# Eighteen steps of a projection moved from a serial phase to a phase of gathers

## The chip, the cores and the metric

The kernel runs on one core of a Trainium2 chip. The metric is the time of one execution on the device in microseconds (us). TensorE is PE in the views (PEld is its weight load), VectorE DVE, ScalarE ACT, GpSimd POOL, SyncE SP.

## The reference

One layer of a streaming encoder for 1024 prompt tokens and 128 sample tokens (8 streams of 16), 1152 in all. Cut to what matters:

```
h  = rms_norm(x, norm1_g);  z = h @ w_in           # columns: rq rk rv rg fq fk fv (512 each), ff (8)
ro = retention(rotary(rq), rotary(rk), rv, state)
fq = rms_norm(fq, fox_qn_g); fk = rms_norm(fk, fox_kn_g); logf = log_sigmoid(ff + b_f)
fo = softmax(fq @ fk.T / 8 + cumulated logf, causal) @ fv
x  = x + concat(norm(ro) * silu(rg), norm(fo)) @ w_out
q  = norm(x) @ wq;  s1, s2 = q halves @ keys       # 8 heads, 2 x 128 keys
e  = the 16 best of the 16 x 16 sums of the 16 best of s1 and of s2;  g = softmax of them
x  = x + sum over 8 x 16 experts of g * gelu(norm(x) . u[e]) * v[e]
```

Outputs are x, the new keys fk, the new values fv, logf and the new retention states. All arithmetic is in float32.

## The kernel before, in words

The 1152 tokens are 9 tiles of 128: tiles 0 to 7 the prompt, tile 8 the samples. The program is a row of phases, each with its own instruction stream for every engine: `phase_norm` (h, transposed, kept in SBUF as `hT`), `projection([RQ, RK, RV])`, `phase_retention`, `projection([RG, FQ, FK, FV])` (the second projection), and `phase_tail`.

A projection takes its groups of 512 columns one after the other and in each the 9 tiles: eight float32 matmuls of 128x512 on PE (L332, each recorded as two passes), and for FQ and FK a square on ACT (L385), a sum per head on DVE (L483), a power on POOL (L418), two multiplications on DVE (L502, L512), and four transposes on PE (L309), copied by ACT. Queries and keys (transposed) go to the scratch tensors `qts` and `kts`, new keys and values to the outputs. The weights of a group (2 MB) sit in one of two buffers. The phase ends when all its stores have landed.

`phase_tail` does everything else, in three groups of three tiles. Its main work is 1152 gathers, each an indirect DMA on POOL's queue (L1256) that brings one row of `peer_uv` (u and v, 8 KB) to each of 128 partitions, into a ring of nine buffers. For each, DVE makes a dot product (L1882); for each four, DVE and ACT make the weights and PE adds the v halves into PSUM (L1641, `yp`), which frees four buffers for POOL. Beside this main work each group has front steps: attention (names fox...), output projection (h...), routing (r...: queries against keys L1594, the best 16 of each half, and the choices `choose`, L1705 on). The choices of a tile end with its indices moved by ACT (L1305); the first gather of the tile waits for these, and the fifth gather of all waits for the last scores of group 0. Groups 1 and 2 are worked among the gathers.

The order is fixed when the program is built. `front_steps` lists the front steps in two threads (`rest` and `choice`) with a cost on each engine and what each needs; `deal` plays a planner's clock in which a gather lands every 2.52 us and puts each step between two items of the main work of its engine. In the second thread each choice is cut in 33 pieces (CAND). The buffers `cand` and `oh` of the choices lie over `fq`, the attention's queries, so `loadq` of group 1 waits until the choices of group 0 are done; attention of group 1 starts after that. SP works through its own list in order: loads, stores, and waits in between.

Of the kernel before, what the change touches and what calls it, by code (L numbers as in the profile page):

```python
# [12 lines left out]
ALU = mybir.AluOpType  # L13
# [19 lines left out]
def emit(nc, a):  # L33

    ctx = ExitStack()
    with ctx:
# [187 lines left out]
        def projection(groups):  # L224
            def body(block, sem, ps):
                steps = [(g, t) for g in groups for t in range(TILES)]
# [10 lines left out]
                if with_ff:  # L237
                    sq_done, ss_done, rs_done, rg_done = sem("sq_done"), sem("ss_done"), sem("rs_done"), sem("rg_done")
                    pool_step, gate_exp, out_done = sem("pool_step"), sem("gate_exp"), sem("out_done")
                    ff_in, ff_done, ff_z, ff_abs = sem("ff_in"), sem("ff_done"), sem("ff_z"), sem("ff_abs")  # L240
# [14 lines left out]
                def _(sp):  # L255
# [9 lines left out]
                    outs = 0  # L265
                    for n, (g, t) in enumerate(steps):
# [29 lines left out]
                    if outs:  # L296
                        sp.wait_ge(out_done, 16 * outs)

                @block.tensor
                def _(pe):  # L300
# [23 lines left out]
                    for n, (g, t) in enumerate(steps):  # L324
                        gi = n // TILES
# [9 lines left out]
                        if t == TILES - 1:  # L335
                            pe.wait_ge(z_done, n + 1)
                            pe.sem_inc(w_used, 1)
# [16 lines left out]
                def _(act):  # L354
# [46 lines left out]
                    if with_ff:  # L401
                        act.wait_ge(tr_done, len(order) + 1)
                        nc.scalar.copy(lgfT[:, 0:NP_TOK], ffpt[:, :, :].rearrange("h a n -> h (a n)")).then_inc(ffT, 1)
                        act.wait_ge(tr_done, len(order) + 2)
                        nc.scalar.copy(lgfT[:, NP_TOK:], ffpt[:, 0, 0:P])
# [298 lines left out]
        CAND = 33  # L704

        def front_steps():
# [7 lines left out]
            def bank(names, engine, name):  # L714
# [4 lines left out]
                return held  # L719

# [37 lines left out]
            for g in range(GROUPS):  # L758
                lo, hi, nt = FIRST[g], FIRST[g + 1], len(tiles_of(g))
                routed = [("pe", ("rscore", g - 1, 4 * GT - 1))] if g else []  # L760
                chosen = [("dve", ("rgate", g - 1, GT - 1))] if g else []
                if nt < GT:
# [91 lines left out]
                for i in range(GT):  # L854
                    top = ("rtop", g, 4 * i + 3 if g == 0 else n - GT + i, 4)
                    for p in range(CAND):
                        add(choice, ("rcand", g, i, p), dve=(1.15, ("dve", top)))
# [9 lines left out]
        def deal(threads):  # L867
# [8 lines left out]
            landed, dots, tanh, freed = [], [], [], []  # L876

# [41 lines left out]
            while True:  # L919
# [20 lines left out]
                if th is not None:  # L940
# [4 lines left out]
                    done[(e, name)] = start + parts[e][0]  # L945
                    continue
                did[e] += 1
                if e == "pool":
                    free[e] = start + 1.25
                    landed.append(max(start + 4.0, (landed[-1] if landed else 0.0) + 2.52))  # L950
# [12 lines left out]
                else:  # L963
                    free[e] = start + 0.1
            assert all(at[e][th] == len(queue[e][th]) for e in engines for th in range(len(threads)))
            return due

        def phase_tail(block, sem, ps):
# [23 lines left out]
            cand = M[:, 34304:36352].rearrange("p (h n) -> p h n", h=PH)  # L992
            oh = M[:, 36352:38400].rearrange("p (k j) -> p k j", j=TOPK)
# [10 lines left out]
            qbd = S[:, 5904:6928].rearrange("p (r b a q) -> p r b a q", r=PAIRS, b=NB, a=2)  # L1004
            ckT = S[:, 6928:7952].rearrange("p (r n) -> p r n", r=PAIRS)
            pn, pns = S[:, 7952:8224], S[:, 8224:8496]
            psT = S[:, 8496:8880].rearrange("p (j m) -> p j m", j=3)
            foT = S[:, 8880:9392].rearrange("p (r n) -> p r n", r=PAIRS)
            lfs, cs, ones_s = S[0:64, 9392:9664], S[0:64, 9664:9936], S[0:64, 9936:10208]
# [17 lines left out]
            ssum = S[:, 5888:5896]  # L1027
            keys2 = S[:, 5904:6928].rearrange("p (s i n) -> p s i n", s=2, i=4)
# [16 lines left out]
            mins = sb("mins", [P, 4])  # L1045
            lsum = sb("lsum", [P, GT, NH])
# [18 lines left out]
            so_mm, so_ev, fT_mm, fT_ev = (sem(x) for x in ("so_mm", "so_ev", "fT_mm", "fT_ev"))  # L1065
            w_in, g2_in = [sem(f"w_in{k}") for k in range(KC)], sem("g2_in")
# [15 lines left out]
            def _(sp):  # L1082
# [9 lines left out]

                def load_wout(g):
# [3 lines left out]
                def front(step):  # L1097
                    kind, g, arg = step[0], step[1], step[2:]
                    if kind == "load":
                        w = (tiles_of(g)[-1] + 1) * P  # L1100
                        if g:
                            sp.wait_ge(s_mm, 4 * GT * g)
                        if len(tiles_of(g)) < GT:
# [917 lines left out]
```

## Time and profile before

| | us |
|---|---|
| median of 3 runs | 4134.53 |
| lowest and highest | 4133.03, 4137.62 |
| the profiled execution | 4142.67 |
| its span (first to last instruction on the core) | 4140.9 |
| mean granted clock of TensorE | 0.731 of full speed |

The profile tells of one execution. Its sections used here are the busy tenths in 40 slices, the queues, the groups of instructions, the windows and the timelines. Times in views count from the start of the span. Busy shares are averages over stages with different limits: up to about 1014 us the engines work through serial phases, after it the gathers run.

### The profile page before, as it was taken

The numbers are of one execution on the slowest core, as the hardware profiler recorded it, in microseconds if no ns is written. First come the engines' busy times: TensorE is split into PE (matmuls) and PEld (weight loads), VectorE is DVE, ScalarE is ACT, GpSimd is POOL, SyncE is SP. The second block draws the span as 40 slices with busy tenths as digits, with TensorE's granted clock in tenths as the row PEclk, the third lists the DMA queues.
The fourth block names the chain that finished last, engine by engine and source line by source line (L and its number), as shares of the span: only waits on it lengthen the run. The fifth ranks groups of instructions, "written<-read, shape, count | busy, mean of one in ns | idle before, by whom it ended". The sixth has DMA issues, their size and how long they took to land.

```text
span 4140.9 us, 34632 instructions
## 1 busy us (share of the span) xinstructions
PE 2460.3 (59%) x11906; PEld 1033.4 (25%) x11906; DVE 2506.7 (61%) x6235; ACT 472.9 (11%) x1311; POOL 1375.9 (33%) x1257
## 2 busy tenths in 40 slices
PE   7998996885337755774753467557734334334333
PEld 3465443442003322321320033123201001001000
DVE  3201720138886655687768766557898875555555
ACT  1000111211002200110110122001101000000000
POOL 0000220001444343433334443433444444444443
PEclk9965997698557777886666588778866565656655
DMA  3001034112999999999989999999999999999999
GB/s 109 21 11 53 21 102 168 69 41 116 420 414 409 421 418 418 394 411 397 413 346 419 416 404 421 420 418 404 412 409 414 418 415 417 421 417 418 416 421 371
DMA packets 242304, 1347.92 MB, mean 326 GB/s; under 512 B 33472, under 2 KB 47624, under 8 KB 94672
## 3 DMA queue, kind: packets, MB, share of 16 engines
q0 software_dynamic: 165888, 1208.03, 70.8%
q1 hardware_dynamic: 73936, 135.34, 8.9%
q10 hardware_dynamic: 2304, 2.32, 0.2%
q8 instruction: 95, 1.56, 0.2%
q14 instruction: 81, 0.66, 0.0%
HBM read 1318.40 MB, written 27.21 MB: 325 GB/s over the span
## 4 chain that ended last, share of the span: by engine, by line
DMA 38%; PE 18%; DVE 14%; POOL 7%; issue 5%; ACT 1%; SPq 1%; another core or an unknown queue 0%; POOLq 0%; DVEq 0%; ACTq 0%
DMA M<-in_peer_uv,M 38%; PE yp L1641 11%; POOL M L1256 7%; DVE M L1882 6%; PE ab L1594 2%; DVE exg L1899 1%; PE ef L1629 1%; DVE strips L1904 1%; PE c L1573 1%; PE d L1480 1%; PE ab L1457 1%; PE d L1573 1%; DVE gel L1891 1%; DVE M L1693 1%; DVE gel L1893 1%
## 5 line engine op out<-in xcount | busy, mean ns | idle before, releaser
L1256 POOL DMA_INDIRECT M<-in_peer_uv,M x1152 | 1294.3, 1123 | 1954.7 <-PE yp L1641 1493.5
L1882 DVE SCALAR_TENSOR_TENSOR M<-M 128x1024 f32<-128x1024 f32 x1152 | 1411.1, 1225 | 870.8 <-DMA M<-in_peer_uv,M 836.2
L1641 PE MATMUL yp<-M,strips 128*32 128x512 f32 x4608 | 927.1, 948 | 1371.1 <-DVE strips L1904 1318.0
L1641 PEld LDWEIGHTS yp<-M,strips 128*32 128x32 f32 x4608 | 161.8, 147 | 2006.2 <-DVE strips L1904 1562.8
L332 PE MATMUL z<-M 128*128 128x512 f32 x1008 | 442.2, 596 | 1.4 <-PEq L104 1.0
L1418 ACT ACTIVATE gel<-gel 128x4 f32<-128x4 f32 x288 | 59.2, 206 | 2233.1 <-DVE gel L1893 2232.5
L1594 PE MATMUL ab<-M 128*128 128x512 f32 x576 | 269.7, 620 | 1.3 <-ACT M L1374 1.3
L332 PEld LDWEIGHTS z<-M 128*128 128x128 f32 x1008 | 189.5, 191 | 226.6 <-issue 226.6
L414 POOL TENSOR_SCALAR small<-small 128x8 f32<-128x8 f32 x27 | 6.1, 227 | 519.5 <-DVE small L483 519.5
L1594 PEld LDWEIGHTS ab<-M 128*128 128x128 f32 x576 | 111.1, 200 | 150.8 <-issue 149.2
L1457 PE MATMUL ab<-M 64*128 64x512 f32 (+3 forms) x192 | 98.2, 627 | 24.1 <-DMA M<-qts_scratch 20.4
L1470 PE MATMUL c<-ident,M 128*128 128x128 f32 x288 | 60.8, 328 | 73.3 <-ACT M L1291 70.7
L1904 DVE SCALAR_TENSOR_TENSOR strips<-gel,exg 128x128 f32<-128x128 f32 x288 | 84.0, 292 | 32.4 <-ACT gel L1418 22.2
L1480 PE MATMUL d<-M 128*64 128x128 f32 x576 | 102.9, 339 | 0.9 <-ACT M L1299 0.9
L1780 DVE CUSTOM_DVE_ANT_0 M<-ab,M 128x896 f32<-128x896 f32 (+6 forms) x64 | 48.2, 755 | 78.2 <-PE ab L1459 59.0
L1882 DVE DVE_READ_ACCUMULATOR M<-M 128x1 f32 x1152 | 94.7, 82 | 0.0
L1899 DVE TENSOR_TENSOR exg<-e,gel 128x128 f32<-128x128 f32 x288 | 84.0, 292 | 10.0
L1480 PEld LDWEIGHTS d<-M 128*64 128x64 f32 x576 | 82.6, 174 | 23.8 <-issue 21.1
L1629 PE MATMUL ef<-ident,M 128*32 128x128 f32 x2304 | 84.7, 296 | 5.8 <-issue 3.8
L1629 PEld LDWEIGHTS ef<-ident,M 128*32 128x32 f32 x2304 | 71.7, 120 | 26.8 <-issue 18.1
L1573 PE MATMUL c<-M 128*128 128x512 f32 x144 | 73.0, 662 | 7.0 <-ACT M L1362 7.0
L1278 ACT ACTIVATE M<-M,mins 128x896 f32<-128x896 f32 (+6 forms) x64 | 49.6, 775 | 227.8 <-DVE mins L1780 227.6
(201 smaller groups left out, 2337.0 us busy)
## 6 DMA issues: line engine op xcount, KB each, us to landing
M<-in_peer_wq SPq DMA_DIRECT2D x12, 2048.0 KB, 31.5
M<-in_peer_uv,M POOLq DMA_INDIRECT x1152
M<-in_w_in SPq DMA_DIRECT2D x7, 2048.0 KB, 9.0
M<-in_w_out SPq DMA_DIRECT2D x24, 512.0 KB, 25.9
M<-in_x_prompt SPq DMA_DIRECT2D x16, 512.0 KB, 7.2
x_scratch<-M SPq DMA_DIRECT2D x9, 512.0 KB, 7.7
xts_scratch<-M SPq DMA_DIRECT2D x9, 512.0 KB, 35.9
M<-xts_scratch SPq DMA_DIRECT2D x9, 512.0 KB
```

The lines of the kernel that those rows point to most:

```text
L332: last = nc.tensor.matmul(z[n % 3][:, :], hT[:, k, t * P:(t + 1) * P], wbuf[:, gi % 2, k, :], start=(k == 0), stop=(k == KC - 1))
L1256: nc.gpsimd.indirect_dma_start(ring[n % NR], None, a["peer_uv"], bass.IndirectOffsetOnAxis(ap=idxH[:, t % 6, s // 4, s % 4:s % 4 + 1], axis=0)
L1457: nc.tensor.matmul(s[:, c:c + w], fq[b0:b0 + 64, r, i * P:(i + 1) * P], kTg[b0:b0 + 64, r, c:c + w], start=True, stop=c + w < width)
L1470: last = nc.tensor.transpose(four(C)[:, j % 4, :], pr[:, n % 3, j * P:(j + 1) * P], ident[:, :])
L1480: last = nc.tensor.matmul(Dk[b0:b0 + 64, 0:P], vg[:, j, h * HD:(h + 1) * HD], pT[:, n % 2, j, :], start=(j == 0), stop=(j == t))
L1573: last = nc.tensor.matmul((C, Dk)[c][:, :], mT[:, t % 2, k, :], wout(g)[:, k, 512 * c:512 * c + 512], start=(k == 0), stop=(k == KC - 1))
L1594: last = nc.tensor.matmul(half_ab[i % 2], xT[:, tt, k, :], wq(g, b)[:, k, :], start=(k == 0), stop=(k == KC - 1))
L1629: last = nc.tensor.matmul(EF[32 * b:32 * b + 32, half, k * P:(k + 1) * P], xTn[:, 4 * half + k, 32 * j:32 * j + 32], ident[:, :], start=Tr ...
L1641: last = nc.tensor.matmul(yp[32 * j:32 * j + 32, 512 * c:512 * c + 512], strips[:, n % 2, j, :], ring[(4 * n + j) % NR][:, D + 512 * c:D + ...
L1882: nc.vector.scalar_tensor_tensor(out=row, in0=row, scalar=1.0, in1=xrep[:, s % 4, :], op0=ALU.mult, op1=ALU.mult, accum_out=dots[:, t % 2, ...
L1899: link(nc.vector.tensor_tensor(exg[:, :, :], bc(e32[:, :].unsqueeze(1), [P, 4, 32]), bc(g[:, 3, :].unsqueeze(2), [P, 4, 32]), ALU.mult))
L1904: nc.vector.scalar_tensor_tensor(out=strips[:, n % 2], in0=bc(g[:, 2, :].unsqueeze(2), [P, 4, 32]), scalar=1.0, in1=exg[:, :, :], op0=ALU. ...
```

## The change

What it does:

- The second projection takes FQ, FK and FV for tiles 0 to 2 alone (`tiles` = 9 for RG, 3 for each of the others). It stores the normalised, transposed rows `hT` of tiles 3 to 8 to a scratch tensor `hts`: six stores of 512 KB on SP, issued behind the load of the last weights; ACT waits for them before it overwrites part of `hT`.
- `phase_tail` gets a new block of front steps, `project`, ahead of the attention of group 1: six tiles by three column groups, 18 steps. It loads the three weight blocks (2 MB each) and the six blocks of `hts` and the two gains again, does the same arithmetic (`pmm` on PE, `pact` on ACT, `psum` and `pnrm` on DVE, `ppow` on POOL, `pturn` on PE and ACT) with two buffers for each intermediate, and stores 6 blocks of `qts`, 6 of `kts`, 6 of new keys and 6 of new values, 256 KB each.
- The load of attention's keys and values for group 1 waits for all of that.
- `cand` and `oh` are halved and lie elsewhere (partly over the routing keys): `choose` handles four heads, then the other four, in 31 pieces. For groups 1 and 2 it waits for the group's last scores. `loadq` of group 1 no longer shares memory with the choices.
- `deal` now adds time to a gather's landing for the bytes that SP's transfers bring (2.4 us per MB by a table).

The diff, cut to its core:

```diff
-        def projection(groups):
+        def projection(groups, tiles):
...
+                    if with_ff:
+                        for t in range(tiles[FV], TILES):
+                            sp.dma_start(a["hts"][t].rearrange("p (k n) -> p k n", k=KC), hT[:, :, t * P:(t + 1) * P]
+                                         ).then_inc(h_out, 16)
...
+            def project(start):
+
+                add(rest, ("pload", 0, 0), sp=(25.0, *start))
+                add(rest, ("pload", 0, 1), sp=(35.0,))
+                for j in range(PJ + 3):
+                    if j < PJ:
+                        q = j // LATE
+                        used = ("dve", ("pnrm", 0, j)) if q < 2 else ("act", ("pact", 0, j))
+                        add(rest, ("pmm", 0, j, 0), pe=(3.8, ("sp", ("pload", 0, q)), *bank("AB"[j % 2], *used)))
+                        add(rest, ("pmm", 0, j, 1), pe=(3.8,))
...
+                if g == 1:
+                    project(routed + [("dve", ("rtop", 0, 4 * GT - 1, 4))])
...
+                    if e == "sp" and landed:
+                        backlog += 2.4 * (mbytes[name[0]] + (4.7 if name[0] in ("hadd", "hxt") and name[2] == GT - 1 else 0.0))
...
+                    other = min(backlog, 2.52)
+                    backlog -= other
+                    landed.append(max(start + 4.0, (landed[-1] if landed else 0.0) + 2.52 + other))
...
+                        sp.dma_start(pw[q % 2], a["w_in"][0, :, (FQ + q) * GW:(FQ + q + 1) * GW]
+                                     .rearrange("(k p) c -> p k c", p=P)).then_inc(pw_in[q % 2], 16)
...
+                    elif kind == "pturn":
+                        m = arg[0]
+                        act.wait_ge(ptr, m + 1)
+                        if m >= 2:
+                            act.wait_ge(pt_out[m % 2], 16 * (m // 2))
+                        nc.scalar.copy(p_turn[m % 2], (C, Dk)[m % 2][:, :]).then_inc(pte, 1)
...
+                        for k in range(4 * half, 4 * half + 4):
+                            last = nc.tensor.matmul(half_ab[j % 2], hTl[i][:, k, :], pw[q % 2][:, k, :],
+                                                    start=(k == 0), stop=(k == KC - 1))
...
-        program(projection([RQ, RK, RV]))
+        program(projection([RQ, RK, RV], [TILES] * 3))
         program(phase_retention)
-        program(projection([RG, FQ, FK, FV]))
+        program(projection([RG, FQ, FK, FV], [0] * 3 + [TILES] + [TILES // 3] * 3))
```

How the order moves. PE, where the gathers begin, before. L1594, L1603 and L1612 are the last routing steps of group 0, L1641 the main work (8 matmuls for each four gathers), L1457 on the attention of group 1:

```order
L1594 MATMUL ab<-M 128x512 x8
L1641 MATMUL yp<-M,strips 32x512 x8
L1603 MATMUL c<-ident,M 128x128 x4
L1612 MATMUL d<-M 128x128 x4
L1641 MATMUL yp<-M,strips 32x512 x168
L1457 MATMUL ab<-M 128x512
L1459 MATMUL ab<-maskq,identb 128x128
```

The same place now. L1644 is `pmm` (4 matmuls for half a step), L1653 `pturn`, L1811 the main work:

```order
L1811 MATMUL yp<-M,strips 32x512 x16
L1644 MATMUL ab<-M 128x512 x12
L1811 MATMUL yp<-M,strips 32x512 x8
L1644 MATMUL ab<-M 128x512 x12
L1653 MATMUL c<-ident,M 128x128 x4
L1644 MATMUL ab<-M 128x512 x4
L1811 MATMUL yp<-M,strips 32x512 x8
L1644 MATMUL ab<-M 128x512 x4
L1653 MATMUL d<-ident,M 128x128 x4
L1644 MATMUL ab<-M 128x512 x4
L1811 MATMUL yp<-M,strips 32x512 x8
```

The 22 main pieces (88 gathers) that stood on PE ahead of the attention of group 1, 21 of them with nothing between, are now 23 (92 gathers), and the 18 steps stand among them.

ACT, around the move of the indices of tile 3, before. L1414 copies the tokens of tile 3 for its dot products and so stands at the end of tile 2; L1305 CAST is the move that gather 384 waits for; L1418 stands once for each four gathers:

```order
L1414 COPY M<-ef 128x512 x6
L1418 ACTIVATE gel<-gel 128x4
L1414 COPY M<-ef 128x512 x2
L1398 ACTIVATE M<-M 128x128
L1305 CAST M<-M 32x32 x16
L1328 COPY M<-ab 128x512 x2
```

The same move now (L1432), with L1565 in the place of L1418; the copies of tile 3 (now L1561) stand twelve main pieces, 48 gathers, further down:

```order
L1565 ACTIVATE gel<-gel 128x4
L1475 COPY M<-ab 128x512 x2
L1482 COPY M<-d 128x256
L1483 COPY M<-d 16x128
L1545 ACTIVATE M<-M 128x128
L1432 CAST M<-M 32x32 x16
L1432 COPY M<-gate 32x32 x16
```

The move came after the last piece of tile 2; now it comes well ahead of it.

## Rows read from the trace of the kernel before

**Rows 1.** The page, span, and busy tenths in 40 slices of 103.5 us.

```profile
span 4140.9 us, 34632 instructions
...
PEclk9965997698557777886666588778866565656655
DMA  3001034112999999999989999999999999999999
```

**Rows 2.** Windows by stage: length, busy us (instructions) of each engine, PE clock, DMA share, GB/s.

```profile
1014.00:1250.00 236.00, 76.92 (x341) 12.86 (x340) 191.25 (x462) 20.70 (x88) 103.16 (x91) 0.58 1.00 412
1250.00:2080.00 830.00, 549.80 (x3053) 243.86 (x3054) 571.46 (x1536) 114.53 (x300) 333.15 (x296) 0.77 1.01 410
2080.00:2100.00 20.00, 14.27 (x247) 11.42 (x245) 9.94 (x25) 11.94 (x40) 3.44 (x4) 0.84 0.23 81
2100.00:4120.00 2020.00, 939.87 (x5293) 301.18 (x5292) 1388.36 (x3360) 173.12 (x542) 863.77 (x770) 0.68 1.01 415
```

**Rows 3.** DMA queues from 1014 us to the end: packets, MB, share of the 16 engines.

```profile
q0 software_dynamic: 165312, 1203.84, 93.4%
q1 hardware_dynamic: 30704, 76.62, 6.4%
```

**Rows 4.** Timeline of PE in the second projection: start, length in us, instruction.

```profile
501.86 7.03 PE L332 MATMUL z<-M 128*128 128x512 f32 x16
508.73 0.60 PE L309 MATMUL ztp<-ident,M 128*128 128x128 f32 x4
509.17 7.03 PE L332 MATMUL z<-M 128*128 128x512 f32 x16
...
627.05 48.23 PE L332 MATMUL z<-M 128*128 128x512 f32 x112
```

**Rows 5.** DMA issues of the page: count, KB each, median us to landing.

```profile
M<-in_peer_wq SPq DMA_DIRECT2D x12, 2048.0 KB, 31.5
...
M<-in_w_in SPq DMA_DIRECT2D x7, 2048.0 KB, 9.0
...
xts_scratch<-M SPq DMA_DIRECT2D x9, 512.0 KB, 35.9
...
M<-x_scratch SPq DMA_DIRECT2D x9, 512.0 KB, 8.2
...
qts_scratch<-M SPq DMA_DIRECT2D x9, 256.0 KB, 5.2
```

**Rows 6.** Short windows around two dips of the DMA share (columns as in rows 2).

```profile
1715.00:1720.00 5.00, 5.00 (x172) 4.36 (x164) 1.40 (x4) 3.37 (x7) 0.00 (x0) 1.00 0.84 347
1720.00:1725.00 5.00, 4.33 (x32) 2.25 (x21) 4.86 (x19) 1.91 (x4) 3.08 (x2) 1.00 0.24 49
...
2080.00:2090.00 10.00, 7.97 (x196) 7.35 (x198) 3.88 (x11) 2.85 (x6) 0.00 (x0) 0.82 0.20 75
2090.00:2100.00 10.00, 6.30 (x62) 4.07 (x51) 6.06 (x14) 9.09 (x35) 3.44 (x4) 0.86 0.27 88
```

**Rows 7.** Timeline of POOL where tile 3's gathers begin; in brackets idle before and releaser.

```profile
2072.93 0.94 POOL L1256 DMA_INDIRECT M<-in_peer_uv,M  x1 [0.30 <-issue]
2095.65 0.94 POOL L1256 DMA_INDIRECT M<-in_peer_uv,M  x1 [21.78 <-ACT M L1305]
```

**Rows 8.** PE groups of 1250 to 2080 us (count, busy us, mean ns), and one busy window.

```profile
L1641 PE MATMUL yp<-M,strips 128*32 128x512 f32 x1168 | 216.5, 879 | 200.9 <-DVE strips L1904 195.1 <-issue 5.7
L1594 PE MATMUL ab<-M 128*128 128x512 f32 x192 | 90.7, 623 | 0.0
...
2650.00:2700.00 50.00, 41.35 (x155) 15.05 (x154) 31.83 (x69) 5.24 (x13) 19.96 (x19) 0.91 1.01 421
```

**Rows 9.** Groups of the second projection's FQ, FK and FV part, 501.4 to 677 us.

```profile
L418 POOL TENSOR_TENSOR small<-small,nhalf 128x8 f32<-128x8 f32 x16 | 26.4, 1648 | 1.3
L512 DVE TENSOR_TENSOR M<-M 128x512 f32<-128x512 f32 x17 | 11.8, 692 | 2.9 <-DVE M L502 0.5
...
L483 DVE TENSOR_REDUCE small<-M 128x8 f32<-128x512 f32 x16 | 11.0, 686 | 43.0 <-ACT M L385 43.0
```

More of the change, by code:

```diff
@@ L222, in emit @@
         RQ, RK, RV, RG, FQ, FK, FV = range(7)
-        def projection(groups):
+        def projection(groups, tiles):
             def body(block, sem, ps):
-                steps = [(g, t) for g in groups for t in range(TILES)]
+                steps = [(g, t) for g in groups for t in range(tiles[g])]
                 turned = [n for n, (g, _) in enumerate(steps) if g in (RQ, RK, FQ, FK)]
@@ L297, in _ @@
                         sp.wait_ge(out_done, 16 * outs)
+                    if with_ff:
+                        sp.wait_ge(h_out, 16 * (TILES - tiles[FV]))
                 @block.tensor
@@ L1098, in front @@
                     kind, g, arg = step[0], step[1], step[2:]
-                    if kind == "load":
+                    if kind == "pload":
+                        q = arg[0]
+                        if q == 0:
+                            sp.wait_ge(s_mm, 4 * GT)
+                            sp.wait_ge(top_done, 4 * GT)
+                        if q == 2:
+                            sp.wait_ge(pz, LATE)
+                        sp.dma_start(pw[q % 2], a["w_in"][0, :, (FQ + q) * GW:(FQ + q + 1) * GW]
+                                     .rearrange("(k p) c -> p k c", p=P)).then_inc(pw_in[q % 2], 16)
+                        if q == 0:
+                            for i in range(LATE):
+                                sp.dma_start(hTl[i].rearrange("p k n -> p (k n)"), a["hts"][GT + i]).then_inc(ph_in, 16)
+                        if q < 2:
+                            sp.dma_start(p_gain[q], a[("fox_qn_g", "fox_kn_g")[q]].rearrange("a h d -> a (h d)")
+                                         .partition_broadcast(P).rearrange("p a c -> p (a c)")).then_inc(pg_in, 16)
+                    elif kind == "pnrm" and arg[0] >= LATE:
+                        sp.wait_ge(pnd, arg[0] + 1)
+                        sp.dma_start(rows("new_fox_k", GT + arg[0] - LATE), p_out[arg[0] % 2]).then_inc(pk_out[arg[0] % 2], 16)
+                    elif kind == "pturn":
+                        m = arg[0]
+                        t = GT + m % LATE
+                        sp.wait_ge(pte, m + 1)
+                        sp.dma_start(a["qts" if m < LATE else "kts"][:, :, t * P:(t + 1) * P],
+                                     p_turn[m % 2].rearrange("p (r n) -> p r n", r=PAIRS)).then_inc(pt_out[m % 2], 16)
+                    elif kind == "pact" and arg[0] >= 2 * LATE:
+                        f = arg[0] - 2 * LATE
+                        sp.wait_ge(pva, f + 1)
+                        sp.dma_start(rows("new_fox_v", GT + f), p_out[f % 2]).then_inc(pv_out[f % 2], 16)
+                    elif kind == "load":
                         w = (tiles_of(g)[-1] + 1) * P
```

220 lines of the change are left out of this document (173 added, 47 removed).

## The prediction

> **What bounds the kernel now.** I read the busy tenths first, then windows by stage, then the DMA queues, then timelines at the two ends of what is moved.
>
> The tenths show two kernels in one [rows 1]. Up to the tenth slice the DMA engines are mostly idle and the engines work in turn; from there on DMA stands at 9 in every slice. The windows confirm it [rows 2]: the 2020 us from 2100 on run at a DMA share of 1.01 and 415 GB/s, the 830 us before at 1.01 and 410, while PE, DVE and POOL all have idle time. So from 1014 us on the limit is bytes: 1203.84 MB by the gathers' queue and 76.62 MB by SP's [rows 3]. An engine's work costs nothing there as long as the gathers stay queued; a MB costs 2.39 us there (418 GB/s, between the rates of full windows, 415 in [rows 2] and 421 in [rows 8]). Before 1014 us it is the reverse: bytes are free and PE's time is the limit. The change moves PE work from the first kind of time to the second, and brings bytes with it.
>
> **What it removes.** In the second projection PE goes from one step to the next without a gap [rows 4]: 7.31 us from one FQ or FK step to the next (501.86 to 509.17, with its transposes), and 48.23 us for the last 112 passes, 16 per step, so 6.89 us for a FV step. Removed are six tiles of each: 12 x 7.31 + 6 x 6.89 = 129.1 us. DVE, ACT and POOL follow PE there (DVE's three ops of a step are 0.69 us each, POOL's power 1.65 [rows 9]), so their share comes off with it. The start of the gathers should move from 1014 to about 885 us: **-129.1 us**.
>
> What could eat into that is the end of the phase, which waits for all stores. SP holds its stores until the weights of FV are issued, which is when FQ is done; PE then has six steps left, 3 x 7.31 + 3 x 6.89 = 42.6 us. In that time go 2.1 MB of weights, the new 3.1 MB of `hts`, 2.4 MB of gated retention rows and 12 blocks of 0.26 MB, 10.8 MB in all. At the rate of the full windows that is 26 us, so I cost it at nothing; the cover is 17 us. A 2 MB load alone takes 9.0 us to land [rows 5], 233 GB/s; were that the rate of all of it, they would need 46 us and 4 us would show.
>
> **What it adds in bytes.** In the gathers' time come three weight blocks of 2.10 MB, six blocks of h of 0.52, two gains of 0.26, and 24 stores of 0.26 MB: 6.29 + 3.15 + 0.52 + 6.29 = 16.25 MB, by 2.39 **+38.9 us**. Below, were some of it to fall into dips of the share that exist anyway, perhaps 33; above, if a step's blocks of 256 KB load the engines less well, 45.
>
> **What it adds in engine work, and what hides it.** The 18 steps stand on PE where 21 main pieces stood alone. That stretch, from the first gathers to attention of group 1, is 1014 to 1250 us: PE busy 76.9 of 236 us, DVE 191.3, ACT 20.7 [rows 2]. It will be four gathers longer (10 us) and 39 us of bytes longer: 285 us. A pass of 128x512 among gathers occupies PE for 90.7 / 192 = 0.47 us [rows 8], so a step 7.6 us and 18 steps 136. The 12 sets of transposes take 0.6 us each at full clock [rows 4], say 11 in all. The 23 main pieces take 216.5 / 73 = 3.0 us each in the next stage [rows 8] and by the row of this one up to 76.9 / 22 = 3.5: 80 us. Sum 227 of 285 us, 80%. DVE gets 12 x 3 x 0.69 = 25 us on top of 191: 76%. POOL issues 91 gathers in 103 us and gets 12 x about 2 us (power, two small ops) more. No engine is full on average, and a window in which PE is 83% busy still has a DMA share of 1.01 [rows 8]. So the work itself is hidden. The chains of it are not quite: a step that waits on an in-order engine holds main work behind it. The nearest row is the dip at 1715 us, where PE worked through other steps and the gathers ran out: 5 x (1.01 - 0.84) + 5 x (1.01 - 0.24) = 4.7 us [rows 6]. I allow two such: **+9.4 us**, with 0 and 48 as bounds (the upper one is the first rival's).
>
> New waits on SP: the first loads wait for the last scores of group 0, which the fifth gather waits for too; behind them on SP nothing is due soon. The load of attention's keys for group 1 now waits for 24 stores, and the wait hides only if the stores land in time; the last rival is about that.
>
> **What it takes away beside that.** Gather 384, the first of tile 3, stands idle 21.78 us for ACT's move of its indices [rows 7], because the order has that move behind the last piece of tile 2; the ring empties and the DMA share falls to 0.20 and 0.27 [rows 6], a loss of 10 x (1.01 - 0.20) + 10 x (1.01 - 0.27) = 15.5 us. In the new order the move comes 12 pieces earlier, some 48 gathers, over 120 us. The wait goes and nothing takes its place at that point, since the whole of group 1 stands earlier too: **-15.5 us**. The choices in two halves keep their operations and their sizes (31 pieces instead of 33, two waits fewer); their new wait for the group's last scores is two routing steps, at the most some 20 us of those 120. Both at nothing.
>
> **Sum**: -129.1 + 38.9 + 9.4 - 15.5 = **-96.3 us**. Against the profiled execution's own 4142.67 that is 4046.4; it is 8.1 us above the median of the three runs, so the median should come to 4134.53 - 96.3 = **4038 us**. A measurement of this kernel can tell about 0.2% (8 us) from no change.
>
> **The rivals.**
>
> 1. *Chains hold up the gathers in the new stretch: about 4077.* A normed step crosses PE, ACT, DVE, POOL, DVE, PE, ACT, SP. DVE's multiplication waits for POOL's power, which stands behind gathers that wait for PE. If each of the 12 costs DVE 4 us (a gather issue and a power, 1.1 + 1.65, and the small ops) that nothing covers, that is 48 us in place of 9.4: 4038 + 39. For it: DVE is the fullest engine there (81%). Against: POOL has more than half its time idle. Chance 0.20.
>
> 2. *PE stays at the low clock: about 4086.* In this stretch TensorE was granted 0.58 on average [rows 2], mostly its lower level of 1.2 GHz, being busy a third of the time. A pass at that level takes twice the 0.43 us of the second projection [rows 4], so a step 13.8 us: 18 steps are 248 us, with transposes and main pieces 342, 57 more than the 285 there are, of which I count 9.4 already: 4038 + 57 - 9.4 = 4086, less a few for passes at the upper level. For it: the stretch has idle gaps of PE between pieces. Against: the busy window of [rows 8] has the same two kinds of work and is granted 0.91. The Trainium skill has a rule for this (TensorE: Matmul & The Clock Gate, section The HAM clock gate): the engine's default is the throttled 1.2 GHz and only sustained activity gives it 2.4. By that rule with the gaps as they were the time would be this rival's; that the granted clock rises from 0.58 to 0.91 as the busy share goes from a third to 83% agrees with its other half, and makes me give it only 0.10.
>
> 3. *The end of the second projection is set by its stores: about 4042*, the 4 us worked out above, inside the forecast's own range. It is also the way in which the change would not do all it says: PE's time is cut and the phase isn't. Chance 0.06.
>
> 4. *Stores set the pace: about 4226, slower than before.* Each intermediate has two buffers, and a step waits for the store of the step but one before. A store under gathers took 35.9 us to land in the rows of `xts` [rows 5]. With 24 stores two at a time that is 12 x 35.9 = 431 us, after some 42 for the first loads (5.5 MB behind one another, by two weight blocks in 31.5 us): 473 in place of 285, 188 more, 4038 + 188 = 4226. It decides from a landing of (285 + 96.3 - 42) / 12 = 28 us on; below that the kernel is still faster. For it: the row. Against: those stores stood behind 4 MB of weights, while lone transfers under gathers land in 8.2 us [rows 5]; and when gathers stop, the stores have the DMA engines to themselves. Chance 0.05.
>
> **How the numbers follow.** The forecast has 0.59, the rivals 0.20, 0.10, 0.06 and 0.05. Its own range is 4020 to 4060. The low end of the whole: bytes at 33, no hold-up, and 10 us of the small dips that SP's heavy loads of group 1 cause now and that may fall away with the new order: 4038 - 6 - 9.4 - 10 = 4012. The high end takes in the first rival and most of the second: 4090. Left out are the last rival and the tails. Faster: all but the last rival and a little for what I don't see, 0.93; no change 0.02; slower 0.05.
>
> **What the new profile should show.** The second projection shorter by 129 us, and the fifth gather issued near 885 us. SP's queue with 93 MB instead of 77 from there on. A stretch of about 285 us from there to attention of group 1, with PE at 75 to 85% and a granted clock over 0.8, and a DMA share of 1.0. No idle time of POOL before gather 384. A granted clock near 0.6 there speaks for the second rival, idle time of DVE ended by POOL for the first, ACT or SP waiting on stores to `qts` or `kts` for the last. The prediction is wrong if the span from the fifth gather to the end grows by over 80 us, or the front shrinks by less than 115.

## The result, and the profile after

| | before | after |
|---|---|---|
| median us | 4134.53 (5 runs) | 4114.70 (5 runs) |
| lowest and highest | 4133.03, 4141.79 | 4105.16, 4119.87 |
| the profiled execution | 4142.67 | 4105.16 |
| its span | 4140.9 | 4103.3 |
| fifth gather issued at | 1014.48 | 879.15 |

The ratio is 0.9942, 95% interval 0.9931 to 0.9954: 20 us faster, where 96 were forecast, and outside the range. Times here and below are medians of a kernel's executions at its ordinary speed; two far slower ones are left out, one of E4 (6852.65 us) and one of E11 (4250.35 us, the one that was profiled). The profiled execution of after lies 9.5 us below its median and that of before 8.1 above, so between the two traces the difference is 37.6 us. Of these, 135.3 were won before the fifth gather, and 97.7 given back behind it (3126.4 us from there to the end of the span before, 3224.2 after). So two questions have to be put to the traces: was the front shortened as forecast, and what lengthened the rest?

The page of after, its span and its tenths, which answer to [rows 1]:

```profile
span 4103.3 us, 34683 instructions
...
PEclk9965967978968787967568787966656565656656
DMA  3001161058999998999999998999999999999999
```

DMA is up in the tenth slice, which stood at 2 in [rows 1], but that slice reads 8, and two more 8s stand in the plateau behind it, where [rows 1] has one.

The front first. On PE's timeline the last block of the second projection (the transposes of `logf`) begins at 675.43 us in before, and in after at 546.34:

```profile
675.43 1.03 PE L348 MATMUL ffpt<-ident,lgf 128*8 128x128 f32 x8
```

```profile
546.34 1.03 PE L356 MATMUL ffpt<-ident,lgf 128*8 128x128 f32 x8
```

That is 129.1 us, the forecast to the tenth; the tenth is luck, for in the traces of some experiments below, with the same code up to there, this block begins some 5 us earlier (670.74 in E7, 540.85 in E8). The first matmul of the tail follows 130.0 us earlier (698.18, 568.16), so the phase's end is still PE's and not its stores'. Another 5.3 us go between there and the fifth gather (316.3 us before, 311.0 after). The windows of this serial piece, of before and then of after (length, busy us and instructions of PE, PEld, DVE, ACT, POOL, clock, DMA share, GB/s), show 4 us less of PE and 6 of DVE. Most of it looks like scatter between executions: the same piece takes 313.3, 313.9 and 314.1 us in the traces of E1, E6 and E7, which move no step, and 314.6, 313.0 and 312.2 in those of E4, E5 and E8, which move all of them.

```profile
698.00:1014.00 316.00, 246.64 (x980) 127.97 (x980) 137.58 (x552) 72.80 (x194) 10.43 (x10) 0.78 0.22 80
```

```profile
568.00:879.00 311.00, 242.61 (x980) 126.42 (x980) 131.37 (x525) 72.95 (x195) 10.14 (x10) 0.80 0.22 83
```

Now the gathers' time. Windows by stage of after, to be held against [rows 2], and its queues from the fifth gather on, against [rows 3]:

```profile
879.15:1199.00 319.85, 195.95 (x689) 72.36 (x689) 225.99 (x536) 37.00 (x119) 142.74 (x127) 0.79 0.94 379
1199.00:4083.00 2884.00, 1493.56 (x8576) 547.49 (x8576) 1966.12 (x4908) 302.30 (x880) 1204.02 (x1063) 0.70 0.99 407
```

```profile
q0 software_dynamic: 165312, 1203.84, 90.8%
q1 hardware_dynamic: 43040, 92.88, 7.6%
```

SP's queue carries 16.26 MB more, as worked out. What was not worked out is the share of 0.94 in the first stretch. Windows of 5 us through the whole time, each taken as its length times (1.01 - share) and as nothing where its share is above 1.01, say how long the DMA engines had nothing to do (the idle DMA time, below): 36.4 us from 1014 to 4120 before, 82.2 us from 879 to 4083 after. That is 46 us more, where 6 less were forecast (9.4 for hold-ups, 15.5 off for the stall at gather 384). With the bytes, some 40 us, it makes 86 of the 97.7. The other 12 come from a little lower rate in the full windows; why it is lower is not shown.

Where the gathers stop, short windows of after:

```profile
945.00:950.00 5.00, 5.00 (x13) 2.18 (x12) 0.77 (x2) 0.60 (x1) 0.00 (x0) 1.00 0.01 3
950.00:955.00 5.00, 4.70 (x23) 1.47 (x22) 4.51 (x11) 0.21 (x1) 3.76 (x4) 1.00 0.00 0
...
970.00:975.00 5.00, 5.00 (x23) 1.62 (x22) 4.40 (x7) 0.00 (x0) 3.83 (x3) 0.94 0.00 0
...
1590.00:1595.00 5.00, 2.36 (x12) 1.99 (x16) 0.00 (x0) 0.27 (x1) 0.00 (x0) 0.50 0.13 50
1595.00:1600.00 5.00, 5.00 (x20) 1.46 (x13) 4.41 (x21) 0.32 (x1) 1.13 (x2) 0.63 0.00 0
```

And what PE did there, its timeline (idle time before and its releaser in brackets; "issue" is a releaser the profile doesn't name):

```profile
939.48 12.45 PE L1644 MATMUL ab<-M 128*128 128x512 f32 x24 [26.70 <-issue]
...
1198.87 2.07 PE L1604 MATMUL ab<-M 64*128 64x512 f32 x2 [14.71 <-DMA M<-qts_scratch]
...
1592.64 2.05 PE L1782 MATMUL d<-M 128*128 128x128 f32 x8 [17.39 <-issue]
...
1824.13 1.97 PE L1681 MATMUL ab<-ident,M 128*128 128x128 f32 x8 [16.84 <-DMA M<-in_cache_fox_k]
...
2521.34 2.05 PE L1782 MATMUL d<-M 128*128 128x128 f32 x8 [16.37 <-issue]
```

Each is the first instruction that needs a load: of the projection (w_in, hts), of attention's queries, of the routing keys, of the cache, and of the routing keys again for group 2. Where the row says "issue", that it was the load is read from the program and from the landing times, not from the row. PE is in order, so main pieces stand behind the waiting step; no `yp` is made, no buffer of the ring of nine comes free, and POOL waits too. On POOL's timeline of after:

```profile
1598.57 0.94 POOL L1383 DMA_INDIRECT M<-in_peer_uv,M  x1 [26.20 <-PE yp L1811]
...
2530.90 0.94 POOL L1383 DMA_INDIRECT M<-in_peer_uv,M  x1 [28.52 <-PE yp L1811]
```

By places, the idle DMA time is 21.4 us at 944 to 979, 9.3 at 1204 to 1219, 14.4 at 1589 to 1619, 2.3 at 1829, 7.6 between 2309 and 2429 (blocks of `w_out`), 12.6 at 2519 to 2534. The routing keys are the telling case, because before had the same load, of the same size, and no wait on it. SP's row of their issue in before, then in after:

```profile
1643.58 5.66 SPq L1179 DMA_DIRECT2D M<-in_keys_t  x2
```

```profile
1563.17 5.65 SPq L1288 DMA_DIRECT2D M<-in_keys_t  x2
```

Before, the first scores that need them started at 1684.03, 40.5 us behind the issue. After, PE asks for them at 1592.64 - 17.39 = 1575.25, 12 us behind the issue, and gets them 29 us behind it. The load isn't slower (the keys' loads of groups 1 and 2 land 34.6 us behind their issue in before and 29.7 in after, medians of four); the order asks for it sooner. Counted in the order of ACT and PE, 16 gathers stood between the last rows of the group and its first scores in before, and 8 stand there now.

### The profile page after: what moved, and what is told of

Its sections match the earlier page's. It is cut to its first block, busy times and chain, and to the rows that moved or that the text cites. A ratio compares the mean times of both kernels' runs of the same rounds, so it can differ in the third digit from the quotient of the medians.

```text
span 4103.3 us, 34683 instructions
## 1 busy us (share of the span) xinstructions
PE 2435.9 (59%) x11906; PEld 1023.0 (25%) x11906; DVE 2506.9 (61%) x6235; ACT 475.9 (12%) x1311; POOL 1395.2 (34%) x1257
## 4 chain that ended last, share of the span: by engine, by line
DMA 35%; PE 20%; DVE 17%; POOL 6%; issue 6%; SPq 2%; ACT 1%; POOLq 0%; DVEq 0%; ACTq 0%
DMA M<-in_peer_uv,M 30%; PE yp L1811 10%; DVE M L2069 7%; POOL M L1383 6%; PE ab L1764 2%; DMA M<-in_w_out 2%; DMA M<-qts_scratch 1%; PE ab L1604 1%; PE d L1627 1%; PE c L1743 1%; DVE exg L2086 1%; DVE strips L2091 1%; PE d L1743 1%; DMA M<-in_w_in 1%; DVE M L1863 1%
## 5 line engine op out<-in xcount | busy, mean ns | idle before, releaser
L1383 POOL DMA_INDIRECT M<-in_peer_uv,M x1152 | 1308.6, 1136 | 1954.1 <-PE yp L1811 1519.6
L1811 PE MATMUL yp<-M,strips 128*32 128x512 f32 x4608 | 906.5, 927 | 1286.0 <-DVE strips L2091 1284.8
L1811 PEld LDWEIGHTS yp<-M,strips 128*32 128x32 f32 x4608 | 159.5, 145 | 1910.9 <-DVE strips L2091 1525.8
L340 PE MATMUL z<-M 128*128 128x512 f32 x720 | 316.6, 597 | 1.4 <-PEq L104 1.0
L1565 ACT ACTIVATE gel<-gel 128x4 f32<-128x4 f32 x288 | 59.2, 206 | 2046.6 <-DVE gel L2080 2046.5
L1764 PE MATMUL ab<-M 128*128 128x512 f32 x576 | 264.4, 610 | 1.3 <-ACT M L1521 1.3
L340 PEld LDWEIGHTS z<-M 128*128 128x128 f32 x720 | 135.8, 192 | 163.5 <-issue 163.5
L1644 PE MATMUL ab<-M 128*128 128x512 f32 x288 | 136.7, 627 | 33.1 <-issue 26.7
L1764 PEld LDWEIGHTS ab<-M 128*128 128x128 f32 x576 | 109.6, 197 | 141.5 <-issue 139.9
L1782 PE MATMUL d<-M 128*128 128x128 f32 x288 | 48.8, 321 | 61.0 <-issue 33.8
L1644 PEld LDWEIGHTS ab<-M 128*128 128x128 f32 x288 | 56.1, 202 | 111.0 <-issue 111.0
```

The costliest lines, as they stand in the source:

```text
L340: last = nc.tensor.matmul(z[n % 3][:, :], hT[:, k, t * P:(t + 1) * P], wbuf[:, gi % 2, k, :], start=(k == 0), stop=(k == KC - 1))
L1383: nc.gpsimd.indirect_dma_start(ring[n % NR], None, a["peer_uv"], bass.IndirectOffsetOnAxis(ap=idxH[:, t % 6, s // 4, s % 4:s % 4 + 1], axis=0)
L1644: last = nc.tensor.matmul(half_ab[j % 2], hTl[i][:, k, :], pw[q % 2][:, k, :], start=(k == 0), stop=(k == KC - 1))
L1764: last = nc.tensor.matmul(half_ab[i % 2], xT[:, tt, k, :], wq(g, b)[:, k, :], start=(k == 0), stop=(k == KC - 1))
L1811: last = nc.tensor.matmul(yp[32 * j:32 * j + 32, 512 * c:512 * c + 512], strips[:, n % 2, j, :], ring[(4 * n + j) % NR][:, D + 512 * c:D + ...
```

## The experiments

**Theory A, the planner's allowances.** `deal` gives each load a fixed time in its clock after which PE may be put on it (40 us for attention's load, 6 for the rows that the keys follow). With the change, the clock also runs on for SP's bytes, by up to a gather's length more per gather. Then the same allowance spans fewer gathers; on the chip the load takes as long as ever, and PE stands at it early. The first two loads of `project` have allowances (25 and 35 us) that are short in themselves. **Its rival**, theory B where an expectation names it: the 18 steps and their 16 MB hold the gathers up by themselves, whatever the allowances. All experiments do the whole computation. Ratios are to the runs of before on the same chip (medians 4135.18 to 4139.08). "Below after" is the distance to the median of after, 4114.70. The executions of one kernel lie within 3 to 19 us of each other, so a distance of some us means little, and a trace can lie several us from its kernel's median.

**E1, the new clock in the kernel before, and nothing else of the change.**

```diff
+                    if e == "sp" and landed:
+                        backlog += 2.4 * (mbytes[name[0]] + (4.7 if name[0] in ("hadd", "hxt") and name[2] == GT - 1 else 0.0))
...
-                    landed.append(max(start + 4.0, (landed[-1] if landed else 0.0) + 2.52))
+                    other = min(backlog, 2.52)
+                    backlog -= other
+                    landed.append(max(start + 4.0, (landed[-1] if landed else 0.0) + 2.52 + other))
...
+                    backlog += 1.2
```

> The kernel before with one part of the change alone: the planner's clock counts SP's bytes. Nothing is moved out of the second projection. Theory A (the new clock packs group 1 and 2 so that loads have fewer gathers to land in, and PE waits for keys, w_out and attention's loads with the main work behind it): new dips of the DMA share of the kind seen in the changed kernel at 1589 and 2519 us (17 us waits of PE for the routing keys), 25 to 35 us of idle DMA more, less the 15.5 us at gather 384 that goes, so 4142 to 4155 us. Theory B (the added loads, stores and steps of the projection are what empties the ring, the clock is innocent): the stall at gather 384 goes and nothing comes, 4117 to 4125 us.

Measured: 4169.05, ratio 1.0084 (1.0071 to 1.0097), 34 us slower, more than A had asked. The waits of after are there without a single moved step, on PE's timeline of E1:

```profile
1608.29 2.04 PE L1620 MATMUL d<-M 128*128 128x128 f32 x8 [17.89 <-issue]
...
2163.43 3.35 PE L1465 MATMUL ab<-M 64*128 64x512 f32 x4 [13.49 <-DMA M<-qts_scratch]
...
2552.81 2.05 PE L1620 MATMUL d<-M 128*128 128x128 f32 x8 [23.91 <-issue]
```

Idle DMA time from 1014 to 4155 is 66.8 us against 36.4: 30 more, though the 15.5 at gather 384 are gone. So the new clock alone costs 34 us, and the DMA time that it loses lies behind waits of A's kind.

**E2, the changed kernel with half the charge.**

```diff
-                        backlog += 2.4 * (mbytes[name[0]] + (4.7 if name[0] in ("hadd", "hxt") and name[2] == GT - 1 else 0.0))
+                        backlog += 1.2 * (mbytes[name[0]] + (4.7 if name[0] in ("hadd", "hxt") and name[2] == GT - 1 else 0.0))
...
-                    backlog += 1.2
+                    backlog += 0.6
```

> The changed kernel with the planner charging half as much time per MB (1.2 instead of 2.4, 0.6 instead of 1.2 for SP's own). The steps stand up to 50 gathers later, 12 gathers instead of 8 between the store of the last transposed tile and the first use of the routing keys. Theory A: the two waits for keys shrink from 17 to under 8 us, 15 to 25 us faster than the changed kernel, 4090 to 4100 us. Theory B: same as the changed kernel, 4110 to 4120 us.

Measured: 4106.54, ratio 0.9928 (0.9916 to 0.994), 8 us below after, between the ranges of A and B. A's waits didn't shrink: the two for the keys are 17.8 and 19.7 us, the first still empties the DMA for 12 us (1659 to 1684), and the total idle is 87.7 us. A smaller charge moves all steps, and the waits turn up elsewhere; this edit doesn't tell the theories apart.

**E3, more room for the first loads alone.**

```diff
-                add(rest, ("pload", 0, 0), sp=(25.0, *start))
-                add(rest, ("pload", 0, 1), sp=(35.0,))
+                add(rest, ("pload", 0, 0), sp=(50.0, *start))
+                add(rest, ("pload", 0, 1), sp=(60.0,))
```

> The changed kernel with the planner's allowance for the projection's first loads at 50 and 60 us in place of 25 and 35. Theory A and B both say that the wait of PE of 27 us at the first projected step goes, with the 21 us of idle DMA behind it: about 4095 us. The rival to both: the ring empties there because 12 matmuls stand between two main pieces, wherever the loads are; then it is the same, 4110 to 4120 us.

Measured: 4090.03, ratio 0.9887 (0.9873 to 0.9901), 24.7 us below after, which rules out the expectation's rival (the same time). The trace shows where, but not as much. The idle time of the first stop is gone (21.4 us), and on PE's timeline the wait of 26.70 is 9.91; but the next wait, for attention's queries, has grown from 14.71, and with it and others the idle DMA time from 879 to 4076 is 82.9 us in all, as much as in after. The spans of the two traces differ by 7.1 us (4103.3, 4096.2), after's being of its fastest execution and E3's of its slowest.

```profile
944.55 6.39 PE L1644 MATMUL ab<-M 128*128 128x512 f32 x8 [9.91 <-issue]
...
1212.52 2.07 PE L1604 MATMUL ab<-M 64*128 64x512 f32 x2 [19.90 <-DMA M<-qts_scratch]
```

**E4, room for all loads.** E3, and for groups 1 and 2:

```diff
-                    add(rest, ("sload", g), sp=(30.0, *routed))
+                    add(rest, ("sload", g), sp=(45.0, *routed))
-                add(rest, ("load", g), sp=(40.0 if g else 12.0, *routed))
+                add(rest, ("load", g), sp=(60.0 if g else 12.0, *routed))
-                add(rest, ("hload", g), sp=(35.0 if g else 12.0, full))
+                add(rest, ("hload", g), sp=(60.0 if g else 12.0, full))
...
-                            act=(1.4, ("pe", ("hxt", g, j))), sp=(6.0, ("act", ("hxt", g, j))))
+                            act=(1.4, ("pe", ("hxt", g, j))), sp=(50.0 if g and j == GT - 1 else 6.0, ("act", ("hxt", g, j))))
```

and the scores (`rscore`) of these groups now need the last `hxt` of SP in the planner's eyes, which they had not.

> The changed kernel with allowances near to the landings seen: first loads 50 and 60 us, attention's keys 60, output weights 60, sample loads 45, and the scores of groups 1 and 2 wait in the plan for the routing keys (50 us after the last transposed tile). Theory A: idle DMA of the gathers' time falls from 82 us to 30 to 40, so 4062 to 4075 us. Theory B: only the first wait goes, 4090 to 4100 us.

Measured: 4050.58, ratio 0.9799 (0.9786 to 0.9812), 64 us below after and 11 faster than even A had asked. Idle DMA time falls from 82.2 to 35.7 us, the level of before. All 18 steps and their bytes are in this kernel, so the rival is out.

**E5 and E9, the parts of E4.** E5 has the keys' two lines alone, E9 the other three loads alone.

> The changed kernel with one allowance alone: the scores of groups 1 and 2 wait in the plan for the routing keys, 50 us after the last transposed tile. Theory A, each late load costs by itself: the two waits of PE for the keys (17 and 16 us, 27 us of idle DMA behind them) go, 4088 to 4095 us. Rival: the lateness only moves to the next load or back to SP's queue (the keys stand behind three stores and two weight blocks), and less than 10 us is won: 4105 to 4115 us.

> The changed kernel with the allowances of attention's keys, output weights and sample loads alone (60, 60, 45 us), the first loads and the routing keys as in the change. With e3_first_wait (-25 us against the changed kernel) and e5_keys_only (-14) this makes the three parts of e4_room (-61). Theory A with parts that add up: -61 + 25 + 14 = -22, 4090 to 4096 us. Rival (a late load hides behind another, so parts give less alone than together): 4098 to 4110 us.

Measured: E5 4100.80, ratio 0.9902 (0.9884 to 0.992), 14 us below after; E9 4093.59, 0.9894 (0.9876 to 0.9911), 21 below, as A asked; E5 lies between A's range and its rival's. With E3's 25 the parts make 60, and E4 together 64, so by the medians they add up. The traces don't bear that out: idle DMA time is 82.9 us in E3, 78.7 in E5 and 74.9 in E9, together 10 below after's 82.2, and E4 is 46 below. What one part wins comes back in part at the next load, as in E3, and only with room for all of them does the idle time go. In E5 the wait of group 1 stayed, though the allowance went from 6 to 50; SP's row of the issue and PE's of the first scores:

```profile
1568.24 5.66 SPq L1288 DMA_DIRECT2D M<-in_keys_t  x2
```

```profile
1603.16 2.05 PE L1782 MATMUL d<-M 128*128 128x128 f32 x8 [19.27 <-issue]
```

They landed 35 us behind the issue and were asked for at 16. 50 us in the slowed clock are not 50 us of the chip; that is A's point, and its size here was underrated.

**E6, the same room in the kernel before, with its old clock.**

> The kernel before, old clock, with the same longer allowances as e4_room (without the projection's). Theory A (before, loads had room already since the planner's clock ran fast): little to win, the stall at gather 384 stays, 4125 to 4140 us. Rival (longer allowances help any order, so e4_room says nothing of the change): 4095 to 4115 us.

Measured: 4154.59, ratio 1.0041 (1.0027 to 1.0054), 18 us slower, which neither theory had. Room isn't free: it puts everything behind the load later, the indices of the next tiles among it. On POOL's timeline the stall of [rows 7] is still there and has a second at gather 768, with 14.0 us of idle DMA time; the total is 50.5 us, 14 more than in before:

```profile
2084.45 0.94 POOL L1256 DMA_INDIRECT M<-in_peer_uv,M  x1 [25.27 <-ACT M L1305]
...
3161.51 0.94 POOL L1256 DMA_INDIRECT M<-in_peer_uv,M  x1 [20.70 <-ACT M L1305]
```

**E7, new clock and room in the kernel before** (E1 and E6 together).

> The kernel before with the new clock (as e1_clock_before, 4169 us) and with the longer allowances. Theory A: the clock hurts only through loads that land late, so the loss goes and the gain of 15 us at gather 384 shows: 4115 to 4128 us. Rival (the denser order itself costs, by engines that run full): 4140 us or more.

Measured: 4135.13, ratio 0.9993 (0.9984 to 1.0002): 34 us below E1, but no faster than before, 7 us above A's range and 5 below its rival's. Its idle DMA time is 32.2 us from 1014 us on. Clock and room belong together: alone, one costs 34 and the other 18 us; together nothing.

**E8, a little more room in the changed kernel**: E4 with 60 for the keys and 60 for `sload`.

> e4_room with 60 us for the routing keys (50) and 60 for the sample loads (45), where its trace still has PE waits of 13.6 and 6.9 us. Theory A: 8 to 12 us less idle DMA, 4042 to 4048 us. Rival: 4053 us, what is left is not late loads.

Measured: 4045.44, ratio 0.9775 (0.9762 to 0.9789), 91 us below before. It beats both kernels. Its tenths, its first stretch, its fifth gather on POOL and its first scores of group 1 on PE:

```profile
DMA  3001161149999999999999999999999999999998
```

```profile
879.00:1199.00 320.00, 205.43 (x748) 73.41 (x752) 244.13 (x565) 37.17 (x122) 160.91 (x136) 0.81 1.01 411
```

```profile
874.73 0.94 POOL L1383 DMA_INDIRECT M<-in_peer_uv,M  x1 [17.83 <-PE d L1782]
```

```profile
1635.46 2.05 PE L1782 MATMUL d<-M 128*128 128x128 f32 x8 [5.97 <-issue]
```

Idle DMA time is 30.3 us from 879 us on. This run also measures the moved steps alone: E7 and E8 have the same clock, almost the same room, no stall at gather 384, and idle DMA times within 2 us (34.0 and 32.2, each from its fifth gather on). E7's fifth gather and its queue of SP from there on, then E8's queue:

```profile
1006.36 0.93 POOL L1264 DMA_INDIRECT M<-in_peer_uv,M  x1 [18.93 <-PE d L1620]
```

```profile
q1 hardware_dynamic: 30704, 76.62, 6.3%
```

```profile
q1 hardware_dynamic: 43040, 92.88, 7.7%
```

The front is 131.6 us shorter (1006.36 to 874.73). From the fifth gather to the end of the span they take 3129.7 and 3171.4 us: 41.7 us for 92.88 - 76.62 = 16.26 MB, 2.56 us per MB. These are single executions, and those of E7 differ by 13 us among themselves, so the price is good to some tenths at best.

**E10 to E12, the charge in E8** (2.4 there): E10 has 1.2 (and 0.6 for 1.2 as in E2), E11 2.0, E12 2.8.

> e8_room3 (4045 us) with the planner charging half per MB. Theory A: with room for the loads the clock matters no more, but the indices of tile 3 now stand behind gather 383 again, as before the change, so the 15 us stall comes back: 4056 to 4064 us. Rival (the clock has a cost or gain of its own beside loads and that stall): outside 4050 to 4068 us.

> e8_room3 with the planner charging 2.0 us per MB in place of 2.4. The move of tile 3's indices stands just behind the last piece of tile 2 again, as in e10_room3_half (4097 us, 1.2 per MB), while the rest of the order is nearly that of e8_room3 (4045). Theory A (of e10's loss, 33 us are the stall at gather 384 and the rest late loads): a stall of POOL of 20 us or more at gather 384, 4062 to 4080 us. Rival (e10 was slow by its looser clock in general): no such stall, 4045 to 4055 us.

> e8_room3 with 2.8 us per MB: front steps denser still, tile 3's indices at gather 356, 12 to 16 gathers between tile and keys as before. Theory A: loads get a little less room (the gathers between are fewer), nothing stalls at 384: 4045 to 4060 us. Rival (the denser the better while allowances are true): under 4042 us.

Measured: E10 4096.80, ratio 0.9895 (0.9877 to 0.9912); E11 4072.73, 0.9844 (0.983 to 0.9857); E12 4059.61, 0.9815 (0.9801 to 0.9828). E10 lies over 30 us above A's range, in its rival's. The stall that the change had removed is back, double, on POOL's timeline at gather 384; the window of it has a DMA share of 0.05. It holds 33.9 of E10's 80.7 us of idle DMA time, where E8 has 32.2 in all, so some 15 us more are lost at other places:

```profile
2022.24 0.94 POOL L1383 DMA_INDIRECT M<-in_peer_uv,M  x1 [44.76 <-ACT M L1432]
```

```profile
1989.00:2024.00 35.00, 19.66 (x292) 14.89 (x292) 24.24 (x48) 11.79 (x38) 1.46 (x2) 0.70 0.05 17
```

So with a fast clock and long allowances the choices fall behind. E11 and E12 are both slower than E8, as A asked. What makes E11's 27 us over E8 isn't shown, since its trace is of the execution of 4250.35 us; that trace does have the stall that A had named:

```profile
2166.92 0.94 POOL L1383 DMA_INDIRECT M<-in_peer_uv,M  x1 [28.51 <-ACT M L1432]
```

Of the four charges tried 2.4 is the best. It is near the 2.56 us per MB just measured, but that this is the reason isn't shown.

## Why the prediction was wrong

**What it removes: right.** 129.1 us forecast, 129.1 measured at PE's last block, 130.0 at the next phase's first matmul, 131.6 from E7 to E8 at the fifth gather. Rival 3 falls with it: the nine last stores of `rets` land in 3.2 us and those of `hts` in 7.4, well within the cover of 17 us.

**What it adds in bytes: right.** 16.25 MB forecast, 16.26 counted; 41.7 us from E7 to E8 against 38.9.

**What it takes away: right at the place.** POOL waits for ACT before gather 384 no more. But "nothing takes its place" was said with the order of ACT before me and not that of PE against SP. 15.5 us went at 2080, and 46 + 15.5 = 61.5 came elsewhere. (That DMA stands at 9 "in every slice" was a misreading of [rows 1]: the slice of that stall reads 8.)

**The step that failed is the allowance of 9.4 us for hold-ups**, with 48 as its upper bound; the traces have 61.5. It was taken from one dip in which PE worked through other steps. It was sized by how busy the engines are, and the question was when loads land. The prediction had the rows for it. Two weight blocks issued together took 31.5 us under the gathers [rows 5], and the first step of `project` needs 5.5 MB; rival 4 even counted 42 us for those, with the planner's allowances of 25 and 35 us in the diff, and then asked only about the stores. In the trace of after SP issues the first of them at 890.12 and PE starts at 939.48, 49 us later. Part of that is SP's own time: its rows of the six blocks of `hts` and of the second gain are long.

```profile
890.12 0.38 SPq L1178 DMA_DIRECT2D M<-in_w_in  x1
890.55 16.07 SPq L1182 DMA_DIRECT2D M<-hts_scratch  x6
...
914.23 22.13 SPq L1184 DMA_DIRECT2D M<-in_fox_kn_g  x1
```

The last of the six blocks is issued at 903.6 and PE starts 36 us behind it, as long as these blocks take to land (35.9 us in the issues of that stretch, below). That is the stop at 944, 21.4 us.

The other 40 us of new idle time have to do with the line on `deal` that the prediction passed over: it told what the charge is and gave it no price. E1 gives it for the kernel before: +34 us, with the waits for the keys and the queries that after has too. How much of the 40 the new clock makes in the changed kernel, and how much the moved steps, isn't shown, since no run has the moved steps with the old clock. E4, with all the room, has 46 us less idle time than after, so room for the loads takes most of the 61.5 away. "Behind them on SP nothing is due soon" was the wrong question too, since it was PE that was put too soon on what SP brings.

**The stretch of 285 us was 320.** The share in it was 0.94 instead of 1.0, some 20 us, and its end is the wait of 14.71 us for attention's queries, in which gathers still ran. PE was busy 196 of 320 us, 61%, not 80. PE's groups of the stretch show which term was off: the passes of the 18 steps took 136.7 us, as counted, but the main pieces 55.9, not 80, because more of them ran at the full clock (2.4 GHz) than in the stages from which I took them: on the timelines 13 of these 22 pieces last about 1.9 us and 7 about 3.6, while in before all 20 whole ones of 1014 to 1250 us last about 3.6, and 21 of 70 between 1250 and 2080 about 1.9.

```profile
L1644 PE MATMUL ab<-M 128*128 128x512 f32 x288 | 136.7, 627 | 33.1 <-issue 26.7 <-DVEq L1950 6.5
L1811 PE MATMUL yp<-M,strips 128*32 128x512 f32 x352 | 55.9, 765 | 76.3 <-DVE strips L2091 76.3
```

The work was hidden even better than forecast, and the loads were not.

**The rivals.** Rival 1 named the right place (chains in the new stretch) and the wrong link. The waits that it was to be seen by, DVE's on POOL's power, are not what stopped the gathers; the main chain there is PE waiting for a load. Rival 2 fell: the granted clock is 0.94 to 1.00 in the three short windows from 945 to 975 above, right after a wait of PE, and 0.79 over the stretch, against 0.58 in [rows 2]. Rival 4 fell: the stores of `qts` and `kts` landed in 13.2 us, the point to decide was 28, and ACT waited for them twice, 16.1 us in all. The page's issues of that stretch show stores and loads side by side:

```profile
M<-in_w_in SPq DMA_DIRECT2D x3, 2048.0 KB, 34.0
M<-hts_scratch SPq DMA_DIRECT2D x6, 512.0 KB, 35.9
...
qts_scratch<-M SPq DMA_DIRECT2D x6, 256.0 KB, 13.2
kts_scratch<-M SPq DMA_DIRECT2D x6, 256.0 KB, 13.2
```

The prediction's own test had it: wrong "if the span from the fifth gather to the end grows by over 80 us". It grew by 97.7. With room given, the moved steps alone are worth -131.6 + 41.7 = -89.9 us between the traces of E7 and E8, where the same two terms of the sum make -129.1 + 38.9 = -90.2. The exchange of PE's time for bytes was sound, and the kernel as built collected 20 us of it, for want of room at the loads.

**What stays open.** How the idle time of after divides between clock and moved steps, why E3, E5 and E9 win more by their medians than their idle times account for, the slightly lower rate in the full windows of after, and why E7 is no faster than before with 4 us less idle time. Room for `hadd`'s stores and a finer table of bytes weren't tried.

## What to carry to other kernels

When an order is fixed by a planner, a change to the planner's clock is a change to every wait in the program: hold each load's issue, its landing in the trace and the first instruction that asks for it side by side, for old loads as well as for the added ones. An allowance for a landing has to be counted in the unit that stands between (gathers here), by the time that the load takes beside that traffic. Too little room stops the in-order engine at the load, too much moves the next tile's indices behind their gathers; both show as the same drained ring, and only the releaser tells them apart.

## What the runs showed of the hardware

SP's queue gets about a third of the bandwidth beside the gathers. Two blocks of `wq`, 4.2 MB together, land in 31.8 us there (median of eight issues of before from 1014 us on), 132 GB/s of the 415 that all move, while 2 MB alone take 9.0 us [rows 5], 233 GB/s. The Trainium skill (DMA: Bandwidth & Descriptors, section Queues, rings and completion order) says that a DMA engine goes round between the queues that have work, a packet at a time. If its packets were those of the queue rows above (1203.84 MB in 165312, 7.3 KB; 92.88 in 43040, 2.2 KB on average), that would be an estimate of 23% for SP; the trace has 32% for these large loads. No run here shows that the profile's packets are the ones meant there, so the figures neither confirm the rule nor contradict it.

The bytes added by SP cost 2.56 us per MB, measured by two kernels that differ by the moved steps and, a little, in room, against 2.39 from the rate of full windows. The scatter between executions is as large as the difference.

SP can take long to get an issue off: under the gathers its row of one gain of 256 KB lasts 22.13 us (at 914.23 us in after), and the six blocks of `hts` take 16.07 us together. What it waits for there the profile doesn't say. A landing counted from SP's turn has to include this.
